# Ten slots of gathered expert rows instead of nine, a descriptor scratch of 4 KB instead of 16 KB, and six gathers ahead of the last attention heads

## The reference

```python
def peer_ffn(h, w_query, sub_keys, expert_u, expert_v):
    ...
    def block(xb):
        q = (xb @ w_query).reshape(tb, PEER_HEADS, 2, PEER_KEY_DIM // 2)
        s = jnp.einsum('thpd,pnd->thpn', q, sub_keys).astype(jnp.float32)
        top_s, top_i = lax.top_k(s, k)
        ...
        best_s, best_j = lax.top_k(cand_s.reshape(tb, PEER_HEADS, k * k), k)
        idx = jnp.take_along_axis(cand_i.reshape(tb, PEER_HEADS, k * k), best_j, axis=-1)
        gate = jax.nn.softmax(best_s, axis=-1)
        u = expert_u[idx]
        act = jax.nn.gelu(jnp.einsum('thkd,td->thk', u, xb).astype(jnp.float32))
        w = (gate * act).astype(xb.dtype)
        return jnp.einsum('thk,thkd->td', w, expert_v[idx])
```

## Time and profile before

| What | us |
|---|---|
| Median of 3 runs (1631.05 to 1642.06) | 1634.97 |
| Span of the profiled execution, first to last instruction | 1623.5 |
| Between the span and the median of the runs | 11.5 |
| TensorE busy | 1363.6 (84%) |
| VectorE busy | 1108.8 (68%) |
| GpSimd busy | 550.4 (34%) |
| Bytes moved by DMA | 617.63 MB, of which gathers 553.68 MB |

### The profile page before, as it was taken

One profiled execution on the slowest core, in us unless ns is written; L12 is line 12 of the kernel. 1 busy time (PEld: TensorE's weight loads), 2 busy tenths in 40 slices (PEclk: granted clock), 3 DMA queues, 4 the chain that ended last, 5 costly groups with the idle time before them and its releaser, 6 DMA issues.

```text
span 1623.5 us, 13929 instructions
## 1 busy us (share of the span) xinstructions
PE 1363.6 (84%) x4002; PEld 653.2 (40%) x4002; DVE 1108.8 (68%) x2844; ACT 423.7 (26%) x1112; POOL 550.4 (34%) x582
## 2 busy tenths in 40 slices
PE   8999898799888698998878689788879787787785
PEld 7744443354333243443335234333335233333332
DVE  1154766777777876668876686877867777777754
ACT  1133222232242223222221223322212222222221
POOL 0034333334343333233343333233333334333341
PEclk9999999999999899999989989799899999999998
DMA  7601999999999999999999999999999999999994
GB/s 270 225 2 52 419 380 409 423 427 391 426 428 427 401 369 419 366 419 399 425 424 423 426 388 419 421 422 396 426 423 374 418 422 427 426 428 426 426 426 197
DMA packets 108097, 617.63 MB, mean 380 GB/s; under 512 B 10955, under 2 KB 11211, under 8 KB 40438
## 3 DMA queue, kind: packets, MB, share of 16 engines
q0 software_dynamic: 76032, 553.68, 82.1%
q1 hardware_dynamic: 31990, 63.05, 10.4%
HBM read 615.65 MB, written 1.05 MB: 380 GB/s over the span
## 4 chain that ended last, share of the span: by engine, by line
PE 45%; DMA 31%; DVE 14%; issue 7%; ACT 2%; POOL 1%; DVEq 0%; SPq 0%; POOLq 0%
DMA arena<-peer_uv,idx 30%; PE bank L1095 25%; PE bank L696 8%; DVE arena L1852 4%; PE bank L735 3%; PE bank L1066 3%; ACT arena L1432 1%; PE bank L837 1%; DVE wgt L1873 1%; DVE pairs L1806 1%; DVE h L1858 1%; DVE top_i L1816 1%; DVE pairs L1834 1%; DVE pairs L1837 1%; DVE picked L1838 1%
## 5 line engine op out<-in xcount | busy, mean ns | idle before, releaser
L1095 PE MATMUL bank<-arena 128*128 128x512 f32 x1944 | 946.9, 636 | 230.6 <-ACT arena L1432 206.9
L1852 DVE CUSTOM_DVE_ANT_0 arena<-arena,bank 128x1024 f32<-128x1024 f32 x528 | 639.8, 1218 | 350.2 <-DMA arena<-peer_uv,idx 346.3
L640 POOL DMA_INDIRECT arena<-peer_uv,idx x528 | 510.4, 967 | 910.8 <-PE bank L1095 874.7
L1095 PEld LDWEIGHTS bank<-arena 128*128 128x128 f32 x1944 | 378.5, 202 | 747.7 <-issue 721.2
L1432 ACT ACTIVATE arena<-con,wgt 128x128 f32<-128x128 f32 x486 | 170.8, 394 | 722.7 <-DVE wgt L1873 711.9
L696 PE MATMUL bank<-wring,hT 128*128 128x512 f32 x304 | 134.7, 596 | 0.0
L1421 ACT ACTIVATE gl<-dots 128x2 f32<-128x2 f32 x264 | 53.6, 203 | 272.3 <-DVE dots L1852 267.1
L696 PEld LDWEIGHTS bank<-wring,hT 128*128 128x128 f32 x304 | 58.1, 192 | 73.1 <-issue 72.4
L1873 DVE SCALAR_TENSOR_TENSOR wgt<-gate_e,z,gl 128x2 f32<-128x2 f32 x264 | 57.5, 218 | 22.5 <-ACT gl L1421 16.5
L1858 DVE SCALAR_TENSOR_TENSOR h<-arena,wgt,h 128x1024 f32<-128x1024 f32 x42 | 54.0, 1285 | 1.5
L1421 ACT ACT_TABLE_LOAD x39 | 50.0, 1283 | 0.7
(11 more groups left out here) (210 smaller groups left out, 895.1 us busy)
## 6 DMA issues: line engine op xcount, KB each, us to landing
wring<-gla_w_in SPq DMA_DIRECT2D x12, 2048.0 KB
arena<-peer_uv,idx POOLq DMA_INDIRECT x528
wring<-gla_w_out SPq DMA_DIRECT2D x4, 2048.0 KB
wring<-peer_w_query SPq DMA_DIRECT2D x4, 2048.0 KB
wring<-attn_w_by_tile SPq DMA_DIRECT2D x3, 2048.0 KB
gws<-peer_w_query SPq DMA_DIRECT2D x2, 2048.0 KB, 12.9
wring<-attn_w_out_by_pair SPq DMA_DIRECT2D x2, 2048.0 KB
hn<-uq_by_kind SPq DMA_DIRECT2D x1, 1152.0 KB, 16.8
```

Of the source, the lines that this page charges most:

```text
L640: nc.gpsimd.indirect_dma_start(out=uvrow[:, n % RING, :], out_offset=None, in_=io["peer_uv"].rearrange("l e d -> (l e) d"), in_offset=bass ...
L1095: last = nc.tensor.matmul(yacc[:, 512 * i:512 * i + 512], wdiag[:, k % DIAGS, :], rows_of(g, k, 1)[:, 512 * i:512 * i + 512], start=first, ...
L1852: v.tensor_tensor_reduce(out=rows, in0=rows, in1=xnow, scale=1.0, scalar=0.0, op0=ALU.mult, op1=ALU.add, accum_out=dots[:, g % 2, k:k + 1] ...
```

## The change

The ring gets a tenth slot. Its 8 KB per partition come out of the descriptor scratch, which shrinks from 16384 to 4096 bytes per partition. `slot_of` turns the ring by one place: gather 0 goes to the last slot, which no longer overlaps the attention's data at all, and gathers 1 to 5 to the five slots that were free early before. So six gathers go out ahead of the wait for `o_taken`. Each gather from the tenth on waits for the one ten places before it.

```diff
-RING = 9
+RING = 10
 DIAGS = 8
-FREE_EARLY = 5
+FREE_EARLY = 6
+SCRATCH = 4096
...
-        assert at >= FREE_EARLY * 2 * D, at
+        assert at >= (FREE_EARLY - 1) * 2 * D, at
...
-        assert at <= RING * 2 * D + DIAGS * P, at
+        assert at <= (RING - 1) * 2 * D, at
...
+        def slot_of(n):
+
+            return (n + RING - 1) % RING
+
         def rows_of(g, k, kind):
 
-            return uvrow[:, (TOPK * g + k) % RING, kind * D:kind * D + D]
+            return uvrow[:, slot_of(TOPK * g + k), kind * D:kind * D + D]
...
                 nc.gpsimd.indirect_dma_start(
-                    out=uvrow[:, n % RING, :], out_offset=None, in_=io["peer_uv"].rearrange("l e d -> (l e) d"),
+                    out=uvrow[:, slot_of(n), :], out_offset=None, in_=io["peer_uv"].rearrange("l e d -> (l e) d"),
...
-    nc = bacc.Bacc("TRN2", target_bir_lowering=False, num_devices=1)
+    nc = bacc.Bacc("TRN2", target_bir_lowering=False, num_devices=1, dynamic_dma_scratch_size=SCRATCH)
```

## The result

The changed kernel takes 1606.13 us (median of 4 runs, 1598.49 to 1612.34), the kernel before on the same chip 1633.01 us (4 runs, 1620.61 to 1642.06). The ratio is **0.9862**, 95% interval 0.9812 to 0.9911: 14 to 31 us faster, 22.5 us by the ratio. The two medians alone give 0.9835, but the four runs of before spread over 21 us; in three later series of 17 to 23 runs the same kernel had medians of 1627.2 to 1627.4 us, and 1606.13 is 0.987 of that, 21 us less. The profiled execution took 1602.71 us with a span of 1600.8 us, 22.7 less than the 1623.5 of before.

A forecast was written before the change was run, and what follows sets the result against it. Row transport at 427 GB/s was taken as the bound, losing time where PE frees slots late. -18.6 (slot) + 1.4 (weights) + 0 (early gather) = -17.2 us, span 1606.3, plus 11.5 around it: 1617.8 us; own range 1612 to 1622, wide 1607 to 1635.

The forecast's parts named there:

- The bound and the lost time: First to last gather: row transport at 427 GB/s bounds; ten stretches where PE falls behind lose 38.0 us.
- One gather a stretch: Tenth slot gains each stretch's loss, at most one transfer of 2.456 us; upper bound 22.8 us, lower 14.5.
- rival 1: PE bounds the stretches, neighbours share one credit: 7 to 12 us gained, 1623 to 1628; 0.35 with rival 4, no effect.
- the middle value, 18.6: Tenth slot's gain in us, taken midway between 14.5 by true idleness and 22.8 by the full cap.
- Rival 3: Extra gather helps more than once in long stretches and weights cost nothing: 27.4 us gained, 1608; chance 0.12.
- The scratch: Shrinking the descriptor scratch costs nothing as long as it holds ten gathers.
- Rival 2: Scratch holds fewer than ten gathers: eight gives +17 us, 1652; only three gives +233; chance 0.05.
- How many must be ahead: Issue to dot takes 6.3 us, so three gathers out feed the engines; the skill's 4.4 us would need two.
- Weight loads: Loads beside gathers land up to 2.456 us later and PE waits: 1.4 us loss, bounds 0 and 4.9.
- The early gather: Sixth gather ahead of the `o_taken` wait gains 0, bounds 0 and 0.5 us; five already keep the queue fed.
- The head: Program start, 154 us, stays; so does the tail after the last gather, 32 us.
- around the span: 11.5 us added to the predicted span of 1606.3 to give the forecast time of 1617.8 us.

The follow-up runs named there:

- half-mix: Second 512 columns of mixes left out except at a row block's first and last pick: kernel before (nine slots) 1608.81 us, changed kernel (ten) 1607.75 us.
- short-query: Layer 0's query projection for the second token block sums 2 of 8 column blocks: kernel before (nine slots) 1623.29 us, changed kernel (ten) 1605.37 us.
- those of the table: Nine slots with 16 (before), 8, 4, 1 KB scratch: ratios 1, 0.9982, 0.9950, 0.9979; ten slots with 8, 4 (changed), 1 KB: 0.9879, 0.9862, 0.9856.

## Why the prediction was right, point by point

**The bound and the lost time.** Right. The half-mix and the short-query runs show it directly: with nine slots and less work for PE, the dips at 216, 366 and 1226 us are at 426 to 427 in the one, and the dip at 366 at 427 in the other. The stretch from 1300 us on is at 427 before and after.

**One gather a stretch.** The cap of 2.456 us holds as a size, not as a law. By the ten stretches the gain in the two profiles is 0.7, 3.5, 2.1, 2.5, 0.5, 2.4, 2.4, 2.6, 2.9 and 2.9 us, five within 0.4 of the cap. But the stretches were picked where the profile of before is low, and the other nine-slot runs are not as low there: with 8 KB the ten lose 27.3 us, not 38.0. Four nine-slot and four ten-slot profiles, those of the table and the one with five early gathers, in windows shifted by as much as each one's first gather is later than at 154.5 us, give a fairer picture. Lost time in us, by the same formula:

| Window, in the time of before | Nine slots, four profiles | Ten slots, four profiles | Gain of the means | Cap as predicted |
|---|---|---|---|---|
| 190 to 250 | 3.2 to 5.2 | 0.3 to 1.4 | 3.7 | 3.2 |
| 350 to 400 | 2.7 to 5.0 | 0.5 to 1.4 | 2.3 | 2.5 |
| 550 to 675 | 13.5 to 14.9 | 9.4 to 11.4 | 4.2 | 7.4 |
| 730 to 755 | 1.6 to 2.5 | 0.3 to 0.4 | 1.8 | 2.5 |
| 925 to 985 | 3.0 to 4.5 | 1.7 to 1.8 | 2.2 | 2.5 |
| 1100 to 1130 | 0.8 to 3.0 | 0.3 to 1.7 | 0.6 | 2.5 |
| 1220 to 1270 | 2.2 to 5.7 | 0.7 to 3.2 | 2.6 | 2.5 |
| 190 to 1270 | 35.4 to 43.0 | 17.7 to 22.8 | 19.0 | |

Four single stretches gain 1.8 to 2.6, near one gather. The first window gains a little more than its cap. From 550 to 675 us neighbouring stretches share a credit, as rival 1 said, but get more than the one that it gave to all three; and the dip near 1108 is hardly there in two of the nine-slot profiles. The seven sum to 17.4 us, against 22.8 at the full cap. So the middle value, 18.6, was near, for reasons that the prediction had only as doubts. Less 1.4 for the weights it gave **17.2 us for the slots, and the runs give 17.4**; an agreement to 0.2 us, where the measured number is known to 3 or 4 and the middle was chosen between 14.5 and 22.8, is luck. Rival 3's total of 1608 us lies nearer to the measured 1606.1 than the forecast does, but it wanted 27.4 us from the slots.

**The scratch.** The term that was wrong is "the scratch costs nothing": it was looked at only for a cost, and it gave 4.9 us, at the end of the program, in a wait that stood in the trace of before (SyncE for PE's sequencer, 5.0 us). The prediction said that the tail stays. Rival 2 falls for 4 KB and for ten slots: with 1 KB they run at 0.9856, and POOL's gathers take 945 ns there in the median, 943 before. By the descriptor sizes of the Trainium skill ("DMA: Bandwidth & Descriptors", terms and the descriptor swizzle), by which the prediction let this rival fall, 1 KB would hold seven gathers, an estimate (1024 bytes / 16 / 9). That the ten-slot kernel isn't slower with it doesn't contradict this: a gather takes 13.5 us from issue to landing in its profile, or 13.5 / 2.456 = 5.5 of them under way. With eleven slots and 1 KB it would be 6.5, and there POOL does fall into the transport's pace, as shown above. So rival 2's mechanism may be real, at a smaller size than 4 KB.

**How many must be ahead.** The first gather is issued at 157.8 and its dot starts at 164.0, 6.2 us, as in the profile before; the Trainium skill's sum of 4.4 is again not what the trace shows. The price of one slot fewer in rival 2, "as one more saves, or somewhat more: +17 us", was far off: eight slots cost 54 us. From the eighth slot to the tenth the gain of a slot fell by more than half.

**Weight loads.** The wait grew as foreseen, at nearly the same place, in TensorE's weight loads of the changed kernel in order of time:

```profile
982.63 0.30 PEld L701 LDWEIGHTS bank<-wring,hT 128*128 128x128 f32 x2 [4.33 <-DMA wring<-gla_w_in]
```

4.33 us against 0.71. The prediction had named waits of several us as a sign of being wrong, and in four profiles each, those of the table above, it is 2.9 to 4.4 us with ten slots and 0.4 to 3.1 with nine. It costs almost nothing yet, as the extra slot covers it: the rate from 980 to 990 us is 425. The 1.4 us booked for it is above what shows, and within the error of the rest. In the kernels with half the mixes and with eleven slots it is 8 to 21 us.

**The early gather**, right at 0. **The head** was said to stay; the first dot was 3.2 us later, which is not the change's (below).

**The number.** 1617.8 was forecast, 1606.1 measured, below the forecast's own range (1612 to 1622) and 0.9 below the low end of the wide one (1607). Of these 11.7 us, the scratch is 5. The rest is the base: 11.5 us were added "around the span", but an execution lies only about 2 us over its span (1602.71 to 1600.8, and 1.8 to 2.5 us in all four runs of the changed kernel). The 11.5 was the difference between a median of three runs, 1635, and a profiled execution that was itself some 9 us quicker; the kernel before measured 1627.2 to 1627.4 in the three later series, of 17, 23 and 17 runs. The difference was well sized, the base it was taken from was not. The marks named in advance came mostly as said: 412 and 407 GB/s at 216 and 366 us (above 390), dips left at 584, 654 and 1108 (now 1100), POOL's wait 842, last gather issued at 1570 (near 1573), 427 late. Two did not: 736 to 750 is gone (421), and 584 to 604 lost only 0.5 us of its dip, not 2.5.

## What to carry to other kernels

A ring in front of a saturated transport pays only where its consumer falls behind, and there by about one transfer for each stretch in which it does; read the stretches by rate, not the engine's wait for slots, which fell by 32 us of 875 here and would promise anything. Here the tenth slot was worth less than half of the ninth, so one fewer costs much more than one more brings. Judge single stretches by several profiles of each kernel, since windows picked at the dips of one profile promise too much. Look also at the resource that pays for a change, and at the last microseconds of the program, for gains as well as costs; and take the time around the span from one and the same execution, never from the median of others.

## What the runs showed of the hardware

**The end of the program.** With the default descriptor scratch of 16 KB SyncE waits 4.7 to 5.0 us for PE's sequencer at the end, with 8, 4 or 1 KB 0.2 us.

**The head goes with the clock.** The same instructions reach the first gather at 154.1 to 165.1 us. From 90 to 150 us the granted clock was, in the kernel before and in the nine-slot run with 1 KB:

```profile
90.00:150.00 60.00, 54.69 (x380) 26.98 (x380) 30.22 (x139) 23.02 (x79) 26.25 (x32) 0.97 0.00 1
```

```profile
90.00:150.00 60.00, 56.71 (x331) 26.07 (x330) 23.16 (x104) 19.54 (x67) 21.12 (x25) 0.77 0.00 1
```

0.97 of 2.4 GHz with the first gather at 154.5, 0.77 with it at 165.1. The nine-slot run with 4 KB has 0.77 and 164.9 too, and most others 0.89 to 0.91 and 156.6 to 159.2. A part of each such window is at the lower level, 1.2 GHz; from 120 to 140 us it is 0.50 in the second profile and 1.00 in the first. The head thus spreads single profiles by 11 us, half of what the change gives.

**A weight load beside gathers.** In the changed kernel the 2 MB loads of `gla_w_in` take 25.6 us from issue to landing:

```profile
wring<-gla_w_in SPq DMA_DIRECT2D x12, 2048.0 KB, 25.6
arena<-peer_uv,idx POOLq DMA_INDIRECT x528, 13.7
```

That is 2.097 MB / 25.6 us = 82 GB/s, a fifth of 427. The queue table gives 63.05 MB / 31990 = 2.0 KB a packet on SyncE's queue, and a gather's rows are 8 KB. With turns one to one in the trace's packets, 2 KB of every 10 would be the weights', 85 GB/s, near the 82; no run here changed a packet's size, so this is not shown. The Trainium skill ("DMA: Bandwidth & Descriptors", queues, rings and completion order) says that a DMA engine takes turns between queues by packets, but its packet is a group of descriptors, typically 9 to 17, while the trace's rows count 9 packets for each engine and gather, so the sum of 85 is not worked out from that rule. Depth matters for other loads: `peer_w_query`, also 2 MB, takes 14.6 us with eight slots, 17.1 to 21.2 in four profiles with nine and full mixes, 28.4 to 32.2 in five with ten and 33.6 with eleven. The `gla_w_in` loads don't follow it, with 22.1 us at eight slots, 23.1 to 26.8 at nine, 22.6 to 25.8 at ten and 25.0 at eleven. So a deeper ring can make weights late, as the prediction feared, as well as PE's faster pace.
